# RWKV preparation with unscaled rate sums: exclusive exponential from the inclusive one, reversed scan, key weights on ScalarE

## The reference, cut to what matters

```python
w_log = -softplus(-(w0 + tanh(wd) @ w_up)) - 0.5
decay = exp(-exp(w_log))              # log decay = -exp(-0.5) * sigmoid(w0 + ...)
a     = sigmoid(a0 + ad @ a_up)
kk    = l2norm(k * k_k)
k_dir = k * (1.0 + (a - 1.0) * k_a)
# per token, state S (v x k):
sa = -S @ kk;  S = S * decay + sa (x) (kk * a) + v (x) k_dir;  o = S @ r
bonus = sum(r * k_d * r_k) * v        # summed over both directions
```

## Time and profile before

| | |
|---|---|
| time, median of 3 runs (range) | 3989.17 us (3984.3 to 3995.16) |
| span of the profiled execution | 3990.6 us |
| busy in the span: PE, DVE, ACT, POOL | 3488.3, 2133.2, 662.1, 791.3 us |
| RWKV preparation, from the first instruction to the next stage's first on PE | 2821.3 to 3232.4 us |
| busy between 2997 and 3040 us (one round): PE, DVE, ACT, POOL | 29.74, 38.61, 14.44, 21.64 us of 43.00 |

### The profile page before, as it was taken

How to read it: one execution, slowest core, us unless ns; L and a number is a source line. 1 busy time by engine, 2 the same in 40 slices (tenths; PEclk the granted TensorE clock), 3 DMA queues, 4 the chain that set the end, 5 groups by cost and what they waited for, 6 DMA issues and landing times. The chain is left out here.

```text
span 3990.6 us, 64126 instructions
## 1 busy us (share of the span) xinstructions
PE 3488.3 (87%) x28192; PEld 2775.3 (70%) x28192; DVE 2133.2 (53%) x2308; ACT 662.1 (17%) x1079; POOL 791.3 (20%) x817
## 2 busy tenths in 40 slices
PE   6999999999998989799999999999567645677798
PEld 3777777777887878688888888876355535676376
DVE  2477777743334555544453353339688835332564
ACT  2122222212000001211110010012233301221100
POOL 0111111111000000034005125000574789000000
PEclk8999999999999999899999999998689867888799
DMA  9444444444332453322232222328478698777243
GB/s 398 143 155 145 163 149 148 151 166 166 119 119 98 176 188 132 114 91 88 84 111 90 85 103 105 125 108 301 130 197 217 165 231 169 180 227 205 69 175 106
DMA packets 359077, 607.72 MB, mean 152 GB/s; under 512 B 136440, under 2 KB 244080, under 8 KB 330128
## 3 DMA queue, kind: packets, MB, share of 16 engines
q1 hardware_dynamic: 305488, 472.23, 37.6%
q0 software_dynamic: 21712, 92.42, 7.1%
q10 hardware_dynamic: 31600, 38.99, 2.8%
HBM read 469.17 MB, written 134.39 MB: 151 GB/s over the span
## 5 line engine op out<-in xcount | busy, mean ns | idle before, releaser
L182 PE MATMUL front_ps<-b_hT,p_wb 128*128 128x512 f32 x4224 | 979.7, 392 | 6.8 <-PEq L94 6.8
L182 PEld LDWEIGHTS front_ps<-b_hT,p_wb 128*128 128x128 f32 x4224 | 790.0, 188 | 187.5 <-issue 20.6
L1772 PE MATMUL in_ps<-b_hT,in_wb 128*128 128x512 f32 (+1 forms) x3264 | 749.7, 390 | 13.4 <-DVE in_wb L1759 13.4
L1772 PEld LDWEIGHTS in_ps<-b_hT,in_wb 128*128 128x128 f32 (+1 forms) x3264 | 606.7, 187 | 147.5 <-DVE in_wb L1759 13.6
L1757 DVE CAST in_wb<-in_raw 128x2048 fp32r<-128x2048 f32 (+1 forms) x68 | 82.7, 1216 | 535.4 <-PE in_ps L1772 530.5
L170 DVE CAST p_wb<-p_raw 128x2048 fp32r<-128x2048 f32 x88 | 108.0, 1227 | 430.5 <-PE front_ps L182 420.2
L813 POOL DMA_DIRECT2D front_mwb<-in_w_ada x128 | 101.3, 796 | 794.8 <-PE front_mps L823 790.0
L1772 PEld LDWEIGHTS in_ps<-b_hc,in_wb 128*128 128x128 f32 (+1 forms) x1728 | 211.4, 189 | 3.2
L1772 PE MATMUL in_ps<-b_hc,in_wb 128*128 128x256 f32 (+1 forms) x1728 | 212.7, 283 | 0.0
L172 DVE TENSOR_TENSOR p_wb<-p_raw,p_wb 128x2048 fp32r<-128x2048 f32 x88 | 201.8, 2293 | 3.0
L1211 PE MATMUL mid_ps<-mid_wb,b_hT 128*128 128x512 f32 x768 | 178.6, 393 | 13.4 <-DVE mid_wb L1196 13.4
(11 more groups left out here) (456 smaller groups left out, 4347.6 us busy)
## 6 DMA issues: line engine op xcount, KB each, us to landing
p_raw<-in_w_in_tiles SPq DMA_DIRECT2D x88, 1024.0 KB, 6.1
in_raw<-in_w_in_tiles SPq DMA_DIRECT2D x67, 1024.0 KB, 4.8
front_mwb<-in_w_ada POOLq DMA_DIRECT2D x128, 512.0 KB, 5.0
open_wb<-in_w_ada_groups SPq DMA_DIRECT2D x32, 1024.0 KB, 11.3
g_scr<-gprep_ob SPq DMA_DIRECT2D x8, 3474.0 KB, 11.6
merge_raw<-in_w_branch_units SPq DMA_DIRECT2D x32, 512.0 KB, 4.6
mid_raw<-in_w_o_parts SPq DMA_DIRECT2D x32, 512.0 KB, 3.7
last_raw<-in_w_out_parts SPq DMA_DIRECT2D x32, 512.0 KB, 3.7
```

The source lines that it names most:

```text
L182: last = self.nc.tensor.matmul(self.ps[:, n % 2, :], self.wb[:, n % 2, x, kt, :], self.hT[:, y, kt, :], start=kt == term == 0, stop=kt == ...
L1772: last = self.nc.tensor.matmul(self.ps[0:width, n % 3, first:end], self.wb[:, n % 2, x, kt, 0:width], h[:, y, kt, :], start=kt == term == ...
```

## The change

1. `add_up`: the sigmoid is summed as it is; the factor -exp(-0.5) goes into the `scale` of the exponentials. For direction 1 the scan runs over reversed views of the tiles, so the sum comes out in its order at once. The exclusive sum rprep_gx is no longer formed. Of 2 (direction 0: 3) or 4 (direction 1) DVE instructions one is left.
2. `exponentials`: two for each direction in place of three. The operand made with the exclusive exponential takes the inclusive one shifted by a token inside each chunk (63 of 64 columns), and one more small copy (12 columns) puts kk itself in the first (last) column.
3. `direct`, new on ACT: 1 + (a - 1) k_a as Identity with a column each for scale and bias, for both directions, after the second sigmoid of rates and before the exponentials. The bias column is made once at the start (`rest`, 8 columns). `operands` keeps one product with the key; it waits for kd_out in place of a_out. rprep_kd has two buffers now, one for each direction.
4. The sum over directions for the bonus is formed in one instruction in direction 1; the copy in direction 0 is gone.

```diff
+    def direct(self, act_e, i, d):
+        if 2 * i + d == 0:
+            act_e.wait_ge(self.s["rest_ok"], 1)
+        if i >= 1:
+            act_e.wait_ge(self.s["ops_ok"], 2 * i)
+        self.alink(self.nc.scalar.activation(self.kd[:, d], self.rate[:, d], ACT.Identity, scale=self.column(5, i), bias=self.rest[:, i:i + 1]))
+        act_e.sem_inc(self.s["kd_out"], 1)
...
     def add_up(self, dve, i, d):
-        gd, gxd, swd, chunks = self.g[:, d], self.gx[:, d], self.sw[:, d], self.chunks
+        order = (lambda x: x[:, ::-1]) if d else (lambda x: x)
         dve.wait_ge(self.s["w_out"], 2 * i + d + 1)
-        self.link(self.nc.vector.tensor_scalar(swd, swd, -math.exp(-0.5), None, ALU.mult))
-        self.link(self.nc.vector.tensor_tensor_scan(gd, self.reset[:], swd, 0.0, ALU.mult, ALU.add))
-        if d == 0:
-            self.tt(gxd, gd, swd, ALU.subtract)
-        else:
-            whole = chunks(gd)[:, :, C - 1:C].to_broadcast([P, NCH, C])
-            self.tt(chunks(gxd), whole, chunks(gd), ALU.subtract)
-            self.tt(gd, gxd, swd, ALU.add)
+        self.link(self.nc.vector.tensor_tensor_scan(order(self.g[:, d]), self.reset[:], order(self.sw[:, d]), 0.0, ALU.mult, ALU.add))
         dve.sem_inc(self.s["g_ok"], 1)
     def exponentials(self, act_e, i, d):
-        self.alink(self.nc.scalar.activation(gx, gx, ACT.Exp))
-        self.alink(self.nc.scalar.activation(ex[:, 0, :], self.g[:, d], ACT.Exp))
-        self.alink(self.nc.scalar.activation(ex[:, 1, :], self.g[:, d], ACT.Exp, scale=-1.0))
+        self.alink(self.nc.scalar.activation(ex[:, 0, :], self.g[:, d], ACT.Exp, scale=-factor))
+        self.alink(self.nc.scalar.activation(ex[:, 1, :], self.g[:, d], ACT.Exp, scale=factor))
     def operands(self, dve, i, d):
-        dve.wait_ge(self.s["a_out"], 2 * i + d + 1)
-        self.link(self.nc.vector.tensor_scalar(kd, rate, -1.0, self.column(5, i), ALU.add, ALU.mult))
-        self.link(self.nc.vector.scalar_tensor_tensor(kd, kd, 1.0, self.k_in[i % 3], ALU.add, ALU.mult))
+        dve.wait_ge(self.s["kd_out"], 2 * i + d + 1)
+        tt(kd, kd, self.k_in[i % 3])
...
-            self.link(self.nc.vector.tensor_copy(ks, kd[:, 0:T]))
-        else:
-            tt(ks, ks, kd[:, 0:T], ALU.add)
+            tt(ks, self.kd[:, 0, 0:T], kd[:, 0:T], ALU.add)
...
-        tt(ob[:, :, self.AR:self.AR + C], chunks(kk), chunks(self.gx[:, d]))
+        to, frm, edge = (slice(0, C - 1), slice(1, C), C - 1) if d else (slice(1, C), slice(0, C - 1), 0)
+        a = ob[:, :, self.AR:self.AR + C]
+        tt(a[:, :, to], chunks(kk)[:, :, to], chunks(ex[:, 0, :])[:, :, frm])
+        self.link(self.nc.vector.tensor_copy(a[:, :, edge:edge + 1], chunks(kk)[:, :, edge:edge + 1]))
...
                         m.rate_gate(act_e, i + 1, 1)
+                        m.direct(act_e, i + 1, 0)
+                        m.direct(act_e, i + 1, 1)
                         m.exponentials(act_e, i + 1, 0)
```

More of the change, by code:

```diff
@@ L2755, in __init__ @@
         self.vt = st.sb("vt", [P, NCH, C])
-        self.gx = st.sb("gx", [P, 2, TA])
         self.ex = st.sb("ex", [P, 2, 2, TA])
-        self.kd = st.sb("kd", [P, TA])
+        self.kd = st.sb("kd", [P, 2, TA])
+        self.rest = st.sb("rest", [P, GW // P])
         self.obs = [st.sb(f"ob{u}", [P, NCH, R_COLS], at=Solver.AT + 18688 + u * 4 * NCH * R_COLS) for u in range(3)]
@@ L2762, in __init__ @@
         self.ps_b = st.ps("ps_b", [P, BANK])
-        names = ("low_ok", "sel_ok", "x_free", "norms", "keyed", "zw", "za", "w_out", "a_out",
+        names = ("low_ok", "sel_ok", "rest_ok", "x_free", "norms", "keyed", "zw", "za", "w_out", "a_out", "kd_out",
                  "g_ok", "exped", "ops_ok", "mb", "mk", "m_out", "tokb", "tokk", "tokv", "b_out", "k_out", "v_out",
@@ L2789, in start @@
         dve.wait_ge(self.given.loaded, 16 * 6)
+        link(nc.vector.tensor_scalar(self.rest[:], self.vec[:, 5], -1.0, 1.0, ALU.mult, ALU.add))
+        dve.sem_inc(self.s["rest_ok"], 1)
     def clear(self, dve, before):
@@ L2850, in exponentials @@
         act_e.wait_ge(self.s["g_ok"], 2 * i + d + 1)
-        gx, ex = self.gx[:, d], self.ex[:, d]
-        self.alink(self.nc.scalar.activation(gx, gx, ACT.Exp))
-        self.alink(self.nc.scalar.activation(ex[:, 0, :], self.g[:, d], ACT.Exp))
-        self.alink(self.nc.scalar.activation(ex[:, 1, :], self.g[:, d], ACT.Exp, scale=-1.0))
+        ex, factor = self.ex[:, d], math.exp(-0.5)
+        self.alink(self.nc.scalar.activation(ex[:, 0, :], self.g[:, d], ACT.Exp, scale=-factor))
+        self.alink(self.nc.scalar.activation(ex[:, 1, :], self.g[:, d], ACT.Exp, scale=factor))
         act_e.sem_inc(self.s["exped"], 1)
@@ L2858, in operands @@
         u, n, ob, chunks, tt = i % 2, 2 * i + d, self.ob(i, d), self.chunks, self.tt
-        kd, bT, kT, ks = self.kd[:], self.bT[:, d], self.kT[:, d], self.ks[:, u]
+        kd, bT, kT, ks = self.kd[:, d], self.bT[:, d], self.kT[:, d], self.ks[:, u]
         ex, rate, kk = self.ex[:, d], self.rate[:, d], self.kk[:, u]
-        dve.wait_ge(self.s["a_out"], 2 * i + d + 1)
-        self.link(self.nc.vector.tensor_scalar(kd, rate, -1.0, self.column(5, i), ALU.add, ALU.mult))
-        self.link(self.nc.vector.scalar_tensor_tensor(kd, kd, 1.0, self.k_in[i % 3], ALU.add, ALU.mult))
+        dve.wait_ge(self.s["kd_out"], 2 * i + d + 1)
+        tt(kd, kd, self.k_in[i % 3])
         if d == 1 and i > 0:
@@ L2870, in operands @@
         tt(kT, kd, ex[:, 1, :])
-        if d == 0:
+        if d == 1:
             if i > 1:
                 dve.wait_ge(self.bonus_st[u], 16 * (i // 2))
-            self.link(self.nc.vector.tensor_copy(ks, kd[:, 0:T]))
-        else:
-            tt(ks, ks, kd[:, 0:T], ALU.add)
+            tt(ks, self.kd[:, 0, 0:T], kd[:, 0:T], ALU.add)
             self.link(self.nc.vector.scalar_tensor_tensor(ks, ks, self.column(6, i), self.r_in[i % 3], ALU.mult, ALU.mult))
```

## The result

The changed kernel took 3966.59 us (median of 4 runs, 3961.41 to 3968.79) beside 3990.28 us for the kernel before: 0.9937 of it, 95% interval 0.9923 to 0.9951. In a second comparison it took 3960.97 us beside 3990.21 (0.9924, 0.9911 to 0.9936). So 24 to 29 us were won; the forecast was 21, 3968 us.

A forecast was written before the change was run, and what follows sets the result against it. POOL's chain was taken as the bound: pairs 0 to 3 stored, then the barrier. Gross 23.5 less 8 gave 15 us at pair 3, some 23 at the barrier, taken as 21: 3968 us, range 3958 to 3982.

The forecast's parts named there:

- First half, 1.4 us a round: DVE's first half of each round: products and a copy go, two edge copies come, saving 1.4 us in every round.
- Second half, t + 8.15: Mask of mk(i,1) begins 8.15 us after t, mk(i,0)'s mask end; saves 6.7 us beside a solve, 1.5 alone.
- ScalarE: ACT trades one exponential for a 1.0 us Identity per direction; hidden, though k_out gains some 0.8 us less than DVE.
- A round alone, 3.4: A whole DVE round with no POOL solve beside it gets 3.4 us shorter.
- Give-back, 8: Rounds 1 and 3, begun earlier, lie deeper under POOL's first two solves; 8 of 23.5 us gross is lost.
- Pair 3 stored 15 us earlier: Net of the first four rounds: the stores that POOL's third solve waits for end 15 us earlier.
- rival B: SP and its transfers set the end, so half the gain is left: 11 us, 3978; chance 0.16.
- The barrier, 21 to 23: POOL resumes behind the barrier ending the preparation some 23 us early; 21 taken, for transfers that crowd.
- signs of being wrong: Two named: POOL's r_mix wait hardly shrinks, or SP's last run of issues, 69.5 us, grows.
- A (lower clock): TensorE runs the second half at 1.2 GHz throughout: about 12 us slower, 4001; chance 0.05.
- C: Freed DVE time turns into waits for PE, only first halves are won: 8 to 9 at the barrier, 3981; chance 0.11.
- D: POOL's third and fourth solves get up to 10 us shorter as DVE blocks POOL less: 3964; chance 0.10.

The follow-up runs named there:

- early pairs: Kernel before with the new code for pairs 0 to 3 only, old code for pairs 4 to 7: 3974.66 us, 0.9966.
- own_wait: Changed kernel with own semaphores for the system transfers, so third and fourth solve each wait only for their direction's systems: 3961.24 us, 0.9914.
- two part runs: Kernel before with only the new rate sums, or only the key weights and the one sum over directions: 3972.69 us and 3979.58 us.
- late pairs: Kernel before with the new code for pairs 4 to 7 only, old code for pairs 0 to 3: 3979.89 us, 0.9974.

## Why the prediction came out right, step by step

**The path: right up to the barrier, and bounded there.** The early pairs move the third solve, the wait for pair 3 shrank from 43.42 to 30.65 us (28 expected; 35.19 in the second profile), TensorE's wait stayed (30.8 and 38.3; 32 expected). That the third solve's start alone does not set the end, own_wait shows.

**First half, 1.4 us a round: right alone, too small beside a solve.** Round 4: 16.85 to 15.49, 1.36 us. Round 0: 31.42 to 27.97, 3.45. The edge copies cost what the row of 48 columns said (1.06 and 0.95 us in round 0), but the step that the products which stay cost as before failed: the one behind the copy fell from 1.57 and 1.54 to 0.69, and without the copies it is back at 1.57 and 1.46. Timeline of DVE in round 0, before and then after:

```profile
2858.73 1.57 DVE L2804 TENSOR_TENSOR rprep_ob<-all_x,rprep_ex 128x512 f32<-128x512 f32 x1
```

```profile
2857.17 1.06 DVE L2886 COPY rprep_ob<-rprep_kk 128x12 f32<-128x12 f32 x1
2858.26 0.69 DVE L2806 TENSOR_TENSOR rprep_ob<-all_x,rprep_ex 128x512 f32<-128x512 f32 x1
```

This is one mis-sized term, 2 us in round 0. A smaller one lies ahead of t: from the mask of mb(0,0) to that of mk(0,0) it was 7.34 us and is 6.29, where the sum had nothing won.

**Second half, t + 8.15: right.** 8.15 or 8.16 in rounds 0 to 5 of the first profile, beside a solve or not, at clock 1.00. That the clock has a part in it is confirmed by itself, at 2.5 us in the profile that the forecast used and 1.5 in the other.

**ScalarE: right.** An Identity takes 1.027 us (1.0 taken), no table load was added (eight and eight in the stage, as before). The last turned keys of pair 3 were ready 6.11 us after the round's end (3027.49 - 3021.38), before 4.51 (3044.64 - 3040.13): 1.6 lost, 0.8 forecast.

**A round alone, 3.4: right, 3.48. Give-back, 8: right in kind.** Rounds 1 and 3 got longer (38.99 to 40.53, 43.23 to 44.40) where 3.4 shorter was the gross gain, 9.5 given back in all, since they now lie deeper under POOL's first two solves. Rounds 0 to 3 together took 193.80 and 194.38 us before, 174.10 and 175.92 after: 19.1 won, 4 more than forecast.

**Pair 3 stored 15 us earlier: right, 15.3, but by two errors that cancel.** The extra 4 us stopped at SP's queue, which the sum left out. Timeline of SP after (store of direction 0, the last load of pair 6, store of direction 1) and ACT's last turned keys, which release it:

```profile
3011.38 1.27 SPq L3000 DMA_DIRECT2D systems<-rprep_ob  x2
...
3031.81 0.71 SPq L2724 DMA_DIRECT2D all_up<-in_rwkv_a_up  x1
3032.62 1.28 SPq L3000 DMA_DIRECT2D systems<-rprep_ob  x2
```

```profile
3026.68 0.81 ACT L2990 ACTIVATE rprep_ob<-rprep_ps_t 128x768 f32<-128x768 f32 x1 [1.84 <-PE rprep_ps_t L2918]
```

The keys were ready at 3027.49; SP, busy without a break since 3011.38, came to the store 5.1 us later. Before, it stood waiting and issued 0.07 us after them (3044.64, 3044.71). This is rival B, in a small part.

**The barrier, 21 to 23: too small, 26.1 by the means, and again with errors that cancel.** POOL reached the barrier 12.2 us earlier by the means, not 15. In the first profile after, its limit and SP's met, as forecast: SP's last issue ends at 3205.38, POOL resumes at 3207.06 after 1.67 us. In the second, SP's last issue ended at 3207.74 and POOL came 4.1 us behind it:

```profile
3213.51 1.02 POOL L2637 TENSOR_TENSOR all_sn<-all_sn 96x462 f32<-96x462 f32 x1 [1.67 <-POOLq L94]
```

On SP's side the mis-sized term is round 5, for which the sum had 8.1 us. It took 33.97 us in place of 53.77 (33.74 and 56.66 in the second profiles): it now begins 6.9 us ahead of the third solve's first instruction, where it had begun 2.2 behind it. Timeline of DVE, begin and end of round 5 before, then the end after (the begin, 3053.56, is shown above):

```profile
3075.79 1.01 DVE L2815 SCALAR_TENSOR_TENSOR rprep_kk<-all_x,all_vec,rprep_ps_n 128x768 f32<-128x768 f32 x1 [0.23 <-DVE rprep_ob L2804]
...
3129.56 1.01 DVE L2815 SCALAR_TENSOR_TENSOR rprep_kk<-all_x,all_vec,rprep_ps_n 128x768 f32<-128x768 f32 x1 [0.23 <-DVE rprep_ob L2804]
```

```profile
3087.53 1.02 DVE L2817 SCALAR_TENSOR_TENSOR rprep_kk<-all_x,all_vec,rprep_ps_n 128x768 f32<-128x768 f32 x1 [0.22 <-DVE rprep_ob L2806]
```

So the store that follows mk(6,0) began 38.7 us earlier, not 23 to 24. But from there to its last issue SP took 81.2 us, 7.0 of them waiting, in place of the 69.5 of the earlier trace rows, and ended 27.1 us earlier. Timeline of SP after, that store and the last issue:

```profile
3124.23 1.27 SPq L3000 DMA_DIRECT2D systems<-rprep_ob  x2
...
3201.74 3.64 SPq L3013 DMA_DIRECT2D r_mix<-rprep_ob  x2
```

Counted in this way SP's last run grew, one of the signs of being wrong; its end came out near the forecast because VectorE had won more than the sum had. And the slack of 9.86 us, from one execution, was taken for a fixed number; it is 21.42 in another.

**The rivals.** A (lower clock) fell: 1.00. C fell with the two part runs. B is real: 5.1 us at pair 3, 8.5 more by the means for the transfers ahead of the third and the fourth solve, 11.6 in SP's last run, and the cap on the late pairs. D fell for the third solve: from its first memset to its store it took 83.1 us before (3073.59 to 3156.70) and 82.9 after (3060.43 to 3143.34). For the fourth it is right in part: the steps ahead of the barrier took 44.5 and 47.4 us before and 39.5 in both profiles after, 6.5 less by the means, with VectorE nearly done. Busy time of PE, PEld, DVE, ACT and POOL over these steps, second profile of before, then after; the same 41 instructions of POOL took 44.23 us beside 34.05 us of VectorE's work and 36.34 beside 1.76:

```profile
3172.66:3220.02 47.36, 26.46 (x434) 24.82 (x434) 34.05 (x25) 9.47 (x12) 44.23 (x41) 0.78 0.92 210
```

```profile
3165.91:3205.39 39.48, 3.07 (x98) 2.82 (x93) 1.76 (x1) 1.62 (x2) 36.34 (x41) 0.60 1.02 229
```

**Slips in the sums that change nothing.** 12 to 27 us off 3989 is 3962 to 3977, not 3961 to 3976; A's terms give 12.7 us, not about 12; D's list of what DVE sheds leaves out the two scalings (0.56 us each, alone).

## What to carry to other kernels

When two engines pass one buffer back and forth, taking work from one of them can bring back the other's clock as well; look at how long the other idles before the slow product, and at the granted clock there. Ask of every gain where it next has to pass (a queue that is already unbroken, a barrier, a load that can start only behind it); a wait that is removed may only uncover the next one (the third solve came 18 to 24 us earlier, the end of the barrier 1 to 11). A slack read from one execution is a sample: here it was 9.86 and 21.42 us in two profiles of the same kernel. And an engine off the path can lengthen the work of the one on it: look at what ran beside it before and after.

## What the runs showed of the hardware that was not expected

A copy of 12 columns took 0.18 us alone and about 1 us beside POOL's solve, and the two-operand product right behind it was then spared: 0.69 us in place of 1.46 to 1.57. The Trainium skill, SBUF — State Buffer, Who interferes with whom, says that such a product contends with GpSimd's reads, and that issue order decides who blocks. The trace agrees that VectorE is held up: the product takes 0.69 us alone. That the wait can fall on the instruction before is what this case shows; why the product goes free behind this copy, but not behind another product, no run here shows.
